# A second transformer block whose attention is spread, step by step, between dense products

## What is computed

```
hx = rmsnorm(x) * (1 + sc1) + sh1;  q, k, v, u, gv, f = split(hx @ w_in)      # and the same for the context rows
attn = softmax([q.k(window of 3 blocks of 128), q.k(256 context keys), sink]) @ [v, cv]     # 8 heads, 2 kv heads
sgu  = gelu(u) * (w_s applied to rmsnorm(gelu(gv)) over 128 tokens)
four = real(fft2(f))
x = x + g1 * rmsnorm(concat(rms(attn), rms(sgu), rms(four)) @ w_out)
x = x + g2 * rmsnorm(relu(hx2 @ w_ff1)**2 @ w_ff2),  hx2 = rmsnorm(x) * (1 + sc2) + sh2
```

## Time and profile before

| | |
|---|---|
| time, median of 3 runs | 4402.12 us (4396.95 to 4403.95) |
| the profiled execution | 4398.56 us, of which its span is 4396.8 us |
| PE busy | 3916.3 us (89%) |
| PEld, weight loads | 3190.6 us (73%) |
| DVE busy | 2095.7 us (48%) |
| ACT busy | 1745.9 us (40%) |
| POOL busy | 1733.5 us (39%) |
| mean granted TensorE clock | 0.940 |

### The profile page before, as it was taken

The page is one execution under the profiler, slowest core; times in us unless marked ns, Lnnn a source line. Parts: engine busy times, 40 slices in busy tenths (PEclk is TensorE's granted clock), DMA queues, the critical chain, the costliest instruction groups (busy, mean ns, idle before and its releaser), DMA issues.

```text
span 4396.8 us, 63048 instructions
## 1 busy us (share of the span) xinstructions
PE 3916.3 (89%) x22940; PEld 3190.6 (73%) x22940; DVE 2095.7 (48%) x2604; ACT 1745.9 (40%) x2893; POOL 1733.5 (39%) x928
## 2 busy tenths in 40 slices
PE   5989999899978879887999999887888888999997
PEld 4767667668656769666787878776778766887886
DVE  5446445455354326556326434636426654347225
ACT  3345354353443435454224323334334543234222
POOL 1434334334323454233444444564345233444443
PEclk8999999999989989888999999998988989999999
DMA  6423333333322230022222222343231022222233
GB/s 229 142 101 133 121 123 128 120 121 124 113 86 92 87 98 12 18 77 72 91 95 87 95 96 91 115 135 104 73 95 29 17 72 72 95 93 90 91 95 110
DMA packets 133593, 422.01 MB, mean 96 GB/s; under 512 B 16784, under 2 KB 27808, under 8 KB 132768
## 3 DMA queue, kind: packets, MB, share of 16 engines
q1 hardware_dynamic: 126352, 408.50, 28.2%
q10 hardware_dynamic: 7056, 10.97, 0.7%
HBM read 397.38 MB, written 6.29 MB: 92 GB/s over the span
## 4 chain that ended last, share of the span: by engine, by line
PE 28%; issue 27%; POOL 8%; DVE 4%; ACT 2%; DMA 1%; POOLq 0%; SPq 0%; ACTq 0%; DVEq 0%
PE lin L2403 12%; POOL wlo L1724 8%; PE lin L2407 7%; PE lin L2591 3%; PE bankT L2571 2%; PE scores L2557 1%; PE scores L2560 1%; DVE tmp L2093 1%; PE lin L2434 1%; DVE tmp L2102 1%; DVE h_lo L2113 1%; DVE a_lo L2297 1%; PE scores L2558 1%; DVE x L2131 0%; DVE h_lo L2266 0%
## 5 line engine op out<-in xcount | busy, mean ns | idle before, releaser
L1724 POOL TENSOR_TENSOR wlo<-wraw,whi 128x1024 fp32r<-128x1024 f32 x454 | 1098.2, 2421 | 1627.7 <-ACT whi L1784 1627.7
L2403 PE MATMUL lin<-h_hi,whi 128*128 128x512 f32 (+1 forms) x2016 | 773.8, 391 | 87.2 <-DVE h_lo L2113 34.0
L1784 ACT ACTIVATE whi<-wraw 128x1024 fp32r<-128x1024 f32 x454 | 477.8, 1056 | 807.0 <-PE lin L2407 575.9
L2403 PE MATMUL lin<-h_lo,whi 128*128 128x512 f32 (+1 forms) x2016 | 747.1, 378 | 0.0
L509 POOL TENSOR_TENSOR wlo<-wraw,whi 128x1024 fp32r<-128x1024 f32 x130 | 314.7, 2421 | 584.4 <-ACT whi L604 584.4
L2403 PEld LDWEIGHTS lin<-h_hi,whi 128*128 128x128 f32 x2016 | 392.4, 195 | 202.9 <-issue 86.2
L2403 PE MATMUL lin<-a_hi,whi 128*128 128x512 f32 (+1 forms) x1280 | 470.9, 375 | 51.8 <-DVE a_lo L2297 43.9
L2407 PE MATMUL lin<-h_hi,wlo 128*128 128x512 f32 (+1 forms) x2016 | 465.4, 374 | 8.5 <-POOL wlo L1724 8.4
L2403 PE MATMUL lin<-a_lo,whi 128*128 128x512 f32 (+1 forms) x1280 | 464.5, 370 | 0.0
L2403 PEld LDWEIGHTS lin<-h_lo,whi 128*128 128x128 f32 x2016 | 395.2, 196 | 67.8 <-issue 7.0
L2407 PEld LDWEIGHTS lin<-h_hi,wlo 128*128 128x128 f32 x2016 | 361.0, 193 | 80.6 <-POOL wlo L1724 15.2
(11 more groups left out here) (332 smaller groups left out, 6242.9 us busy)
## 6 DMA issues: line engine op xcount, KB each, us to landing
wraw<-in_w SPq DMA_DIRECT2D x544, 512.0 KB, 3.7
mod_ring<-in_w_ada SPq DMA_DIRECT2D x96, 512.0 KB, 4.7
mod_ring<-in_w_mod SPq DMA_DIRECT2D x32, 512.0 KB, 4.7
wraw<-in_dft_tokens SPq DMA_DIRECT2D x32, 512.0 KB, 3.2
turn<-turn SPq DMA_DIRECT2D x144, 64.0 KB, 2.1
first_ring<-in_w_mod SPq DMA_DIRECT2D x16, 512.0 KB, 17.1
q_swap<-q SPq DMA_DIRECT2D x36, 128.0 KB, 2.4
x<-in_x ACTq DMA_DIRECT2D x2, 2048.0 KB, 21.4
```

What stands on the lines that cost most here:

```text
L1724: nc.gpsimd.tensor_tensor(wlo[:, s, 0:D], wraw[:, s, 0:D], whi[:, s, 0:D].bitcast(F32), ALU.subtract)\
L1784: nc.scalar.activation(whi[:, s, 0:D], wraw[:, s, 0:D], ACT.Copy).then_inc(*w_hi.one)
L2403: nc.tensor.matmul(bank[s][:, 0:p.w], whi[:, s, k * P:(k + 1) * P], h[:, k, 0:p.w], start=(k == 0 and h is hi), stop=False)
```

## The change

- **Attention in steps.** A step `i` is one query block and one pair of heads (one of each kv head). Between dense chunks TensorE does `begin` (scores of step i, values of step i-2), then, inside the chunk, `turn` of the first head of step i-1, and behind it that of the second. In layer 0 there are 40 steps (32 latent, 8 context), in layer 1 32. They lie in the 12 chunks of row 1's projection (steps 0 to 11), in two slots of the `dims` products, in 16 slots of the DFT (one DFT chunk each), and in the first chunks of `merge`. The stage `attend` is gone.
- **Form of a step.** Scores are float32 products of 64 partitions, one kv head on each half; no split queries and keys, no swaps by DMA, no work of GpSimd. VectorE takes one maximum over both heads (2 x 640), multiplies the probabilities by the reciprocal before the transposes (two operations on 128 x 640, new), and values come out transposed already, into `bankO`. There is one PSUM area for scores.
- **Order of rows.** The context is projected second (layer 0: rows 0, context, 1), and first in layer 1 (context, 0, 1); feed-forward of layer 0 goes 0, context, 1. Keys and values are the first chunks of a row.
- **Norms into staged rows.** `scale` writes all 8 blocks to a new buffer `staged` (for `merge`, onto the mixed rows in place) during the last chunks of the row before, so at the start of a row only `high` and `low` are left. Sums of squares are taken earlier too.
- **Pairs.** `high_pair` gives the first two chunks of a row, and of each return from the hidden units, together: four products for each `k` that arrives, instead of two.
- **Rotary turn.** The product with `rot` is replaced by four DMA transfers of 32 x 512 within SBUF for each of 10 chunks a layer (`turned_half`), issued by SP between the weight loads.

```diff
-GV2, U2, Q2, K2, F2, V2 = 0, 2, 4, 8, 9, 11
+V2, K2, GV2, U2, Q2, F2 = 0, 1, 2, 4, 6, 10
...
+IN_ROWS, MERGE_ROWS, FF_ROWS = [[0, NB, 1], [NB, 0, 1]], [[0, 1, NB], [0, 1]], [[0, NB, 1], [0, 1]]
...
+LATENT_STEPS = SEQ // P * 4
+STEPS2 = [LATENT_STEPS + CTX // P * 4, LATENT_STEPS]
+STEP_AT = [0, STEPS2[0]]
+DIM_POINT, DFT_POINT = IN2, IN2 + 2
+MERGE_POINT = DFT_POINT + DFT
...
+        def scaled_at(n, kind, k):
+            p = n.rows
+            if kind == "mix":
+                return mixed(p, k)
+            return tmp[:, 2 + k % 2, 0:p.w] if p.context and p.l else staged[:, k, 0:p.w]
...
+            def turned_half(r):
+                sp.wait_ge(*rope_raw.after(0, r + 1))
+                for half in range(2):
+                    for n in range(2):
+                        to, at = 64 * half + 32 * n, 64 * half + 32 - 32 * n
+                        sp.dma_start(tmp[to:to + 32, 4 + r % 2, :], tmp[at:at + 32, 6 + r % 2, :]).then_inc(rope_turned[r % 2].sem, 16)
...
+            def attend(l, i):
+                if i < STEPS2[l]:
+                    tile, g = step_of(l, i)
+                    no, n = STEP_AT[l] + i, sum(blocks_of(tile)) * P
+                    act.wait_ge(*nm_ready.after(no, 1))
+                    if i < 2:
+                        act.wait_ge(*norms["pre"]["ready"].after(pre_mix(l, 1).no, KB))
+                    else:
+                        act.wait_ge(*pt_done.after(2 * (no - 1), 0))
+                    for kv in range(2):
+                        nc.scalar.activation(probs[i % 2][:, kv, 0:n], score_cols(tile, kv), ACT.Exp, scale=ATT_SCALE,
+                                             bias=nmax[:, i % 2, kv:kv + 1], accum_out=esum[:, i % 2, kv:kv + 1])
+                    nc.scalar.activation(esink[:, i % 2, :], sink_arg[:, i % 2, :], ACT.Exp).then_inc(*exp_done.one)
+                turned(l, i - 1, 0)
...
+                tile, g = step_of(l, i)
+                no, r = STEP_AT[l] + i, i % 2
+                dve.wait_ge(*s_ready.after(no, 1))
+                link(nc.vector.reduce_max(mx[:, r, :], both_scores(tile), AX_X))
+                sink = neg_sink[:, l, 2 * g:2 * g + 2]
+                link(nc.vector.scalar_tensor_tensor(nmax[:, r, :], mx[:, r, :], -ATT_SCALE, sink, ALU.mult, ALU.min))
+                nc.vector.tensor_tensor(sink_arg[:, r, :], nmax[:, r, :], sink, ALU.subtract).then_inc(*nm_ready.one)
...
+            def normalize(l, i):
+                if i >= STEPS2[l]:
+                    return
+                r, n = i % 2, sum(blocks_of(step_of(l, i)[0])) * P
+                dve.wait_ge(*exp_done.after(STEP_AT[l] + i, 1))
+                link(nc.vector.tensor_tensor(esum[:, r, :], esum[:, r, :], esink[:, r, :], ALU.add))
+                link(nc.vector.reciprocal(rden[:, r, :], esum[:, r, :]))
+                for kv in range(2):
+                    nc.vector.tensor_scalar(probs[r][:, kv, 0:n], probs[r][:, kv, 0:n], rden[:, r, kv:kv + 1], None, ALU.mult)\
+                      .then_inc(*pn_ready.one)
...
+            def high_pair(g, p, parts, when):
+                for k in range(KB):
+                    high_products(g, 0, p, parts, [k], when)
+                    high_products(g + 1, 1, p, parts, [k])
...
+            def begin(l, i):
+                if i < STEPS2[l]:
+                    score(l, i)
+                if 0 <= i - 2 < STEPS2[l]:
+                    values(l, i - 2)
...
+                for kv in range(2):
+                    nc.tensor.matmul(local[kv], t["identb"][:], band, start=True, stop=False)
+                nc.tensor.matmul(distant[0], queries[0], keys[rows[0], 0:CTX], start=True, stop=True).then_inc(*s_far.one)
+                nc.tensor.matmul(local[1], queries[1], near[rows[1], :], start=False, stop=True)
+                nc.tensor.matmul(local[0], queries[0], near[rows[0], :], start=False, stop=True)
+                pe.wait_ge(*s_far.after(LATENT_STEPS * l + i, 1))
+                nc.tensor.matmul(distant[1], queries[1], keys[rows[1], 0:CTX], start=True, stop=True).then_inc(*s_ready.one)
...
+                        last = nc.tensor.matmul(bankO[half, g * P:(g + 1) * P], v, probsT[:, kv, at:at + P],
+                                                start=(k == 0), stop=(k == n - 1))
...
+                    if h % 2 == 0:
+                        pe.wait_ge(*w_hi.after(g, 2))
+                        passes(0, h_hi, whi, (0, 1))
+                        if h == 12:
+                            sum_mix(first, 2)
+                        turn(l, i - 1, 0, also)
+                        passes(1, h_lo, whi, (0,))
+                    else:
+                        passes(1, h_lo, whi, (1,))
+                        turn(l, i - 1, 0)
+                        pe.wait_ge(*w_split.after(g, 2))
+                        passes(2, h_hi, wlo, (0, 1)).then_inc(lin_done.sem, 2)
+                    turn(l, i - 1, 1)
...
-                            pe.wait_ge(*w_hi.after(g + 2 * part, 2))
-                            passes(0, h_hi, whi)
-                            passes(1, h_lo, whi)
-                            pe.wait_ge(*w_split.after(g + 2 * part, 2))
-                            passes(2, h_hi, wlo).then_inc(lin_done.sem, 2)
...
+                def outputs(g, grp):
+                    high_pair(g, p, a_parts, lambda k: a_ready.after(grp, k + 1))
+                    low_products(g, 0, p, a_parts)
...
-                        for n, k in enumerate(parts):
-                            nc.tensor.matmul(local, q_parts[:, r, kv, :], k[:, kv, keys], start=(n == 0), stop=False)
-                        nc.tensor.matmul(local, t["identb"][:], mask[:, mask_no, :], start=False, stop=True)
-                    for n, k in enumerate(parts):
-                        last = nc.tensor.matmul(scores[kv][:, 4 * P:4 * P + CTX], q_parts[:, r, kv, :], k[:, kv, 0:CTX],
-                                                start=(n == 0), stop=(n == 1))
...
-                    nc.tensor.matmul(bank[4 + r % 2], rot[:], tmp[:, 6 + r % 2, :], start=True, stop=True)\
-                      .then_inc(*rope_mm.one)
```

More of the change, by code:

```diff
@@ L1800, in residual_square @@
-            def residual_square(n, k, buffers):
+                if not first and done:
+                    act.wait_ge(*sig["add"].after(n.no, done))
+                nc.scalar.activation(tmp[:, totals[part] if first else slot, 0:w], src, ACT.Square).then_inc(*sig["sq"].one)
+            def residual_square(n, k):
                 if n.after:
                     act.wait_ge(*updated.after(n.after.no, k + 1))
-                square("pre", n, k, buffers, residual(n.rows, k))
-            def roots(kind, n, dsts, banks, widths):
+                square("pre", n, k, pre_sums(n), residual(n.rows, k))
@@ new lines, in gelus @@
+            def gelus(p):
+                act.wait_ge(*lin_free.after(p.in_at + U2 + 1, EVACUATED))
+                for s in range(2):
+                    part = gvn[:, 2 * s:2 * s + 2, :].rearrange("p t n -> p (t n)") if not p.context else gvn[:, s, :]
+                    nc.scalar.activation(part, part, ACT.Gelu_apprx_tanh).then_inc(*gv_in.one)
+                for c in range(2):
+                    nc.scalar.activation(u[:, c, p.cols], u[:, c, p.cols], ACT.Gelu_apprx_tanh).then_inc(*gv_in.one)
@@ L2141, in project, with attend @@
+            def attend(l, i):
+                turned(l, i - 1, 0)
+                normalize(l, i)
+            def project(l, p):
+                n, nxt, attending = pre_mix(l, p.b), next_in(l, p.b), p.b == 1
+                if p.in_no and not (l and p.context):
+                    for k in range(KB):
+                        low("pre", n, k)
+                if l and p.context:
                     return
```

1438 lines of the change are left out of this document (721 added, 717 removed).

## The result

The changed kernel takes 4268.8 us (median of 4 runs, 4268.0 to 4272.9) against 4403.0 us (4 runs, 4397.0 to 4405.6): ratio 0.970, 95% interval 0.9685 to 0.9714. It is faster, by 134 us and not by the 300 forecast, and lies above the range. Its profiled execution has a span of 4270.7 us.

A forecast was written before the change was run, and what follows sets the result against it. TensorE, though unevenly, with time lost at hand-overs. Savings of 140 us in layer 0, 123 in layer 1 and 57 in feed-forward took the profiled 4398.6 to 4079; 20 added gave 4100 us, range 4035 to 4215 (8 in 10).

The forecast's parts named there:

- the step and the overlap: Attention steps on TensorE: 4.5 us for a pair of heads side by side; a row 1 projection slot 9.9 us.
- The heads overlap: Denies a rival, 1 in 10: heads don't overlap, a step costs 7.1 instead of 4.5 us, +134 us, 4235.
- nothing turned serial: Denies a rival, 0.5 in 10: slots become chunk plus the whole chain, +506 us, 4610.
- the DFT, 16 x 8.4 + 4 = 138 us: Layer 0's 16 DFT slots with one attention step each, set by VectorE and ScalarE at 8.4 us, plus 4.
- the chain of 8.4 us: VectorE and ScalarE per attention step: maximum, exponentials, normalization at 1.0 us per operation, copies and hand-overs, 8.4 us.
- The rival of blocking behind GpSimd: Normalization waits for a GpSimd split in each step, DFT slots grow by 2.4 us; about 100 us, 4200; 2 in 10.
- the merge, 168 + 110 us: Merge of layers 0 and 1, down from 183 and 132 us, with context attention steps at 2 us each.
- the feed-forward, -57 us: Both layers: returns -23, first chunks -6.5 twice, three row changes -4.5 each, layer boundary -8.
- this very effect for the DFT: Before each DFT pair, a 2.18 us wait for whi: both ring slots used, next weights unrounded until the last product.
- the projections, 249 + 214 us: Projections of layers 0 and 1 with attention in row 1's twelve slots; 231 and 194 us before.
- about 3 us of idleness: Row starts: with rows already scaled and chunks paired, about 3 us idle stay per start and the pacing goes.
- The 20 us of margin: Added to the sum of 4079 us for unforeseen waits in some 60 slots where four engines must meet.

The follow-up runs named there:

- combined: Changed kernel with additions, copies and next-row scales reordered, returns from hidden units in blocks, and tensors at multiples of 128 bytes: 4168.4 us, 0.9466.
- no_ctx_steps: Changed kernel without the context's eight attention steps in layer 0: 4233.1 us, 0.9613.
- adds_first: Changed kernel with VectorE's additions of squares in the projections moved ahead of the same slot's rotation: 4259.6 us, 0.9673.
- The five edits: Changed kernel, one edit each: additions before rotations, additions behind attention, copies first, returns in blocks, tensors at 128-byte multiples: 9, 25, 13, 25, 19 us saved.
- two_slots: The kernel combined plus a second buffer for squares in the projections and the mixing norm's sums: 4161.8 us, 0.9453.
- place_192: Changed kernel with q, u, f, a_hi and a_lo moved to 192 bytes above a multiple of 256: 4255.8 us.
- place_96: Changed kernel with q, u, f, a_hi and a_lo moved to 96 bytes above a multiple of 256: 4266.9 us.
- weights_moved: As aligned, but rounded weights whi and wlo moved from 128 bytes above a multiple of 256 to a multiple of 256: 4297.2 us.
- aligned: Changed kernel with ms made 96 bytes longer, so q, u, f, a_hi and a_lo start at multiples of 128 bytes: 4250.2 us, 0.9651.
- shifted: Changed kernel with ms made 32 bytes longer, so the tensors behind it start at odd multiples of 64 bytes: 4267.5 us, 0.9686.
- before_aligned: Kernel before the change with ms made 64 bytes longer, so the tensors behind it start at multiples of 128 bytes: 4411.7 us, 1.0021.

## Why the prediction was right, and where it failed

**Right: the step and the overlap.** The pieces of a step take 4.3 us (4.5 worked out), projection slots 9.74 (9.9). The heads overlap, and nothing turned serial. The 2.18 us idle ahead of the DFT's products is gone. The rotary transfers did not make the weights late: ScalarE waited 107.1 us for `wraw` in this part of the program before and 82.1 after.

**Right by luck: the DFT, 16 x 8.4 + 4 = 138 us.** The 16 slots take 137.5 us in layer 0 (1614.77 to 1752.24) and 137.6 in layer 1, and this is a sum of two errors. The first nine average 7.7 us: the normalization was overestimated, and with 2 x 0.61 us for 2 x 1.0 the chain of 8.4 us comes to 7.6. The three with sums of squares take 11.2, beyond the 10 us that the prediction named as a sign of being wrong: VectorE stands for ScalarE's squares ahead of the copy that TensorE needs. With the additions moved and the rest of combined the 16 slots take 127.4 us.

**The rival of blocking behind GpSimd** did not happen in each step. In five of the 72 steps the two normalizing operations take 2.5 to 2.9 us together, else about 1.0 or less; the median of L2177 is 548 ns, its longest 2401. The Trainium skill (SBUF — State Buffer, Who interferes with whom) says that such an instruction can be blocked for the whole of GpSimd's; the longest fits that, the mean shows how seldom. The row that the prediction read for this rival, L2297, is of another kind, with two inputs in SBUF, and it is operations of that kind that lost time here: a scale of a row has a median of 746 ns, a mean of 1446 and a longest of 2954, which is 22 us more in 48 scales than in the kernel before. GpSimd's splits run beside the slow ones (1461.34 to 1466.70 us at the start of row 1). No run takes the splits away, so what they cost at row starts is not shown.

**Failed: the merge, 168 + 110 us.** This is the largest miss, 90 us. The sum had TensorE's work, 2 us for a context step, and "VectorE's updates and squares crowd there", sized as work. The step that failed is that a merge slot is the dense chunk plus TensorE's pieces. A context step costs 4.5 us (no_ctx_steps, 20 us more for eight), and the order of additions and copies 38 us (25 and 13, a part of it in the DFT); the two overlap, since the waits of the wrong order stand in the context's slots too. A likely reading, not tested by itself, is that a step with small products has waits of the same number as a large one: transposes, copy, transposes, copy, values, and short products leave less to hide them. What the rest is made of, no run separated. The single waits of up to 8.0 us at the sums and 8.5 us for `h_lo` are in it, but they are not new: in layer 0's merges TensorE waited 18.2 us for sums before and 10.0 after.

**Failed: the feed-forward, -57 us.** The step "16 returns of 512 tokens lose 1.43 us each now, covered by the pair: -23" looked at one side of the pair: it needs both chunks' weights at once, and with two ring slots the second is rounded only when the last hidden chunk is finished. The prediction had described this very effect for the DFT and did not apply it here. Measured, pairing is worth some 5 us at the returns and 6 us at the starts, neither clear of noise; in blocks the returns alone are worth 29 (4273.4 to 4244.1). On top, 128 chunks x (5.62 - 5.49) = 17 us were lost to the places of `a_hi` and `a_lo`, which no row read from the trace before shows.

**Failed: the projections, 249 + 214 us, by 43.** Row 0 was costed at "8 for gate, turned values and refilled banks", with nothing for the sum in slot 9, and the rotary transfers "at nothing", on the ground that they don't hold up the weights. They hold up VectorE instead (4.13 us at 1373.65), the additions stand behind it, and TensorE waits 6.59 us for the sum; adds_first returns 9 us. The row starts were to keep "about 3 us of idleness", with "rows already scaled". The scales were not done in time: from 1313 to 3600 us TensorE waits 53.6 us for low parts, 14 times, which is 3.8 on average and up to 8.5, with products at the lower clock behind.

**The 20 us of margin** stood for unforeseen waits. The five edits alone found 91 us of such waits and places.

The changed kernel is 169 us above the forecast. The edits of two_slots take 107 of them back (4268.8 to 4161.8), 19 by places alone. For the other 62 I can say only where TensorE waits: in combined, 43.3 us for rounded weights (34 times), 34.5 us for `h_lo` at starts (10 times) and 24.9 us for sums in `bankT` (7 times). Waits for sums were 49.9 us in the kernel before and are 47.3 in the changed one: taking the squares earlier did not remove them.

## What to carry to other kernels

When work is interleaved between engines that run in program order, write for each slot the order of every engine side by side, and look for one that waits for a late result ahead of an early one: here three such moves were worth 9, 25 and 13 us without a change of work. A stage whose total fits may still hold two errors; compare its slots one by one. A pair or group of chunks moves a wait to whatever the second member needs; price both members. After changing any allocation, compare the spacing of unchanged instructions in the two traces before explaining a difference by the change.

## What the hardware showed that was not expected

The spacing of chunks of 24 products of 512 columns depends on where weights and moving operand lie in SBUF. Starts are bytes above a multiple of 256, by the allocation in the compiled programs; the last figure of each row is read from the timelines. place_192, place_96 and weights_moved have one run each.

| kernel | `whi`, `wlo` | moving operand | us per chunk |
|---|---|---|---|
| all with `h_hi`, and aligned | 128 | 128 | 5.44 |
| place_192, and the kernel before | 128 | 192 | 5.49 |
| place_96, shifted, before_aligned | 128 | 96, 64, 0 | 5.60 |
| the changed kernel | 128 | 32 | 5.62 |
| weights_moved | 0 | 128 | 5.57 |

That weights_moved slows the chunks over `h_hi` too, whose operand did not move, shows that it isn't the moving operand's place alone. Equal places, both at 128, gave the fastest chunk, and 192, the place of before, gave before's 5.49 again. Whether the rule is the difference of the two (both at 0 wasn't tried), and what in the chip causes it, stays open. The Trainium skill (SBUF — State Buffer, Who interferes with whom) gives TensorE two independent read ports, one for moving operands and one for weights; by that the places would be nothing to each other, and the rows differ by 3%.

Small operations on VectorE are not safe from long ones: L2150, two columns, has a median of 216 ns and a longest of 2078, which is near the 2.4 us of GpSimd's split. The one at 1678.97 us ends at 1681.05, and GpSimd's two splits there run from 1676.33 to 1681.03. The ends agree; that it waits for the split is not tested.
